# Three gate units of each layer moved from the search stage into the stage of the key scores

## What is computed

```python
h = x @ w_in                                   # (1024, 1024) @ (1024, IN_WIDTH), split in 14 parts
sc = einsum('bqhd,bsd->bqhs', qi, ki)          # key search: 8 index heads of width 64, 1024 keys
idx_score = einsum('bqhs,bqh->bqs', relu(sc), wi)
_, idx = lax.top_k(where(causal, idx_score, -inf), 256)
...                                            # attention over the 256 keys found, two further attentions
mixed = concatenate([a, bo, co]) * silu(gate)  # gate: 1024 columns of h
out = mixed @ w_out;  x = layer_norm(ALPHA * x + out)
```

## Time and profile before

| | us |
|---|---|
| median of 3 runs (lowest, highest) | 3095.87 (3090.37, 3101.58) |
| the profiled execution, its span | 3091.31, 3089.6 |
| PE busy (share of the span) | 2838.9 (92%) |
| DVE busy | 1642.1 (53%) |
| ACT busy | 984.2 (32%) |
| POOL busy | 792.1 (26%) |
| score stage, layer 1 and 2 (1475.3 to 1541.8, 2344.8 to 2411.3) | 66.5, 66.5 |
| search stage, layer 1, from its first product to its last | 261.3 |

### The profile page before, as it was taken

One profiled execution on the slowest core, in us unless ns is written; L12 is line 12 of the kernel. 1 busy time (PEld: TensorE's weight loads), 2 busy tenths in 40 slices (PEclk: granted clock), 3 DMA queues, 4 the chain that ended last, 5 costly groups with the idle time before them and its releaser, 6 DMA issues. The chain is left out here.

```text
span 3089.6 us, 39183 instructions
## 1 busy us (share of the span) xinstructions
PE 2838.9 (92%) x14936; PEld 2312.0 (75%) x14936; DVE 1642.1 (53%) x2808; ACT 984.2 (32%) x1911; POOL 792.1 (26%) x510
## 2 busy tenths in 40 slices
PE   5999888989999999989699989988898899999988
PEld 4777687778888888868378878776685688778767
DVE  4270476533224224233799536676435996265866
ACT  3150454121001001110574034564104660244741
POOL 2233103213333333423033351002131233340021
PEclk9999898999999999999999999999899999999999
DMA  3101002111121121132032520005320224300042
GB/s 111 38 31 51 2 1 87 61 36 44 38 69 38 39 68 48 41 134 55 9 113 92 139 101 1 1 1 174 127 64 11 96 96 123 136 1 1 1 137 96
DMA packets 83146, 194.07 MB, mean 63 GB/s; under 512 B 15488, under 2 KB 34448, under 8 KB 81936
## 3 DMA queue, kind: packets, MB, share of 16 engines
q1 hardware_dynamic: 71056, 153.78, 14.9%
q10 hardware_dynamic: 11904, 37.76, 4.0%
HBM read 141.18 MB, written 33.55 MB: 57 GB/s over the span
## 5 line engine op out<-in xcount | busy, mean ns | idle before, releaser
L344 PE MATMUL psum<-H,ffn_W 128*128 128x512 f32 x672 | 262.9, 391 | 4.8 <-DVEq L1716 3.1
L345 PE MATMUL psum<-H,ffn_W 128*128 128x512 f32 x672 | 262.4, 390 | 0.0
L346 PE MATMUL psum<-H,ffn_W 128*128 128x512 f32 x672 | 262.4, 390 | 0.0
L344 PE MATMUL psum<-H,tk_W 128*128 128x512 f32 x640 | 249.2, 389 | 0.4 <-POOL tk_W L2045 0.4
L346 PE MATMUL psum<-H,tk_W 128*128 128x512 f32 x640 | 249.0, 389 | 0.0
L345 PE MATMUL psum<-H,tk_W 128*128 128x512 f32 x640 | 249.0, 389 | 0.0
L1483 POOL CAST ffn_W<-ffn_W 128x1024 fp32r<-128x1024 f32 (+1 forms) x77 | 65.1, 846 | 471.3 <-PE psum L346 469.1
L1963 DVE TENSOR_SCALAR_CACHE_REDUCE MB<-OM,tk_mid 128x512 bf16<-128x512 f32 (+2 forms) x192 | 184.3, 1010 | 2.3
L1931 ACT ACTIVATE MB<-OM,tk_mid 128x384 bf16<-128x384 f32 (+2 forms) x192 | 157.2, 820 | 74.0 <-DVE tk_mid L1960 73.2
L2043 POOL CAST tk_W<-tk_W 128x1024 fp32r<-128x1024 f32 (+1 forms) x56 | 54.3, 970 | 482.7 <-PE psum L346 331.4
L1697 DVE TENSOR_SCALAR ffn_Y<-ffn_G,ffn_par 128x1024 f32<-128x1024 f32 x21 | 21.1, 1004 | 288.6 <-ACT ffn_G L1670 288.6
(11 more groups left out here) (443 smaller groups left out, 7193.7 us busy)
## 6 DMA issues: line engine op xcount, KB each, us to landing
tk_W<-in_w_feat SPq DMA_DIRECT2D x40, 512.0 KB, 3.6
ffn_W<-in_ffn_w_gate SPq DMA_DIRECT2D x21, 512.0 KB, 3.6
ffn_W<-in_ffn_w_val SPq DMA_DIRECT2D x21, 512.0 KB, 3.5
ffn_W<-in_ffn_w_down SPq DMA_DIRECT2D x42, 256.0 KB, 2.6
OM<-in_w_feat SPq DMA_DIRECT2D x16, 512.0 KB, 7.3
OM<-MB ACTq DMA_DIRECT2D x64, 128.0 KB, 2.4
GATE<-OM ACTq DMA_DIRECT2D x16, 512.0 KB, 3.3
OM<-OM ACTq DMA_DIRECT2D x64, 128.0 KB, 3.3
```

The costliest lines, as they stand in the source:

```text
L344: pe.matmul(out, a1, b1, start=start, stop=False)
L345: pe.matmul(out, a1, b2, start=False, stop=False)
L346: return pe.matmul(out, a2, b1, start=False, stop=stop)
```

## The change

Three of the eight gate units are no longer made in the search stage. The score stage gets them: SP loads their three weight tiles ahead of the small parameters, POOL splits them, and PE does a unit's 48 matmuls in 16 chunks of three, put behind score steps of at most 512 keys (two heads each). The scores use six single banks (three steps in flight in place of two pairs of heads), the unit the fourth pair. ACT bends each step by itself, and after the step behind a unit's last chunk it takes the unit's Silu and sends it to DRAM; PE's next unit waits for that Silu. In the search stage DVE puts the selection of one query tile behind each of the first six rotary units; the swap of halves has one buffer pair instead of two.

```diff
+GATES_BESIDE = 3

-def index_stage(kit, IQ, VS, IS, AM, causal, prepare):
+def index_stage(kit, IQ, VS, IS, AM, causal, prepare, XT, rest, items, staged, GATE, first):
-    SLOTS = 4
+    H, SLOTS, PAIRS, PARTS, UNIT_PAIR, CHUNKS = 8, 4, 3, 2, 3, 2 * KT
+    U = len(items)
...
+    steps = [(t, h, c) for t in range(NT) for h in range(0, H, 2) for c in range(0, P * (t + 1), HALF)]
+    bent_by = [2 * max(s for s, (tt, hh, _) in enumerate(steps) if (tt, hh) == (t, h - h % 2)) + h % 2 + 1
+               for t, h in heads]
+    share = [end_of(t, c) - c for t, h, c in steps[:-4]]
+    upto, last_step, n = [], [], 0
+    for s in range(len(steps)):
+        while n < min(CHUNKS * U, CHUNKS * U * sum(share[:s + 1]) // sum(share)):
+            if n and n % CHUNKS == 0 and s < last_step[-1] + 2:
+                break
+            n += 1
+            if n % CHUNKS == 0:
+                last_step.append(s)
+        upto.append(n)
...
             def _(sp):
+                for i, src in enumerate(items):
+                    if i >= PARTS:
+                        sp.wait_ge(split, i - PARTS + 1)
+                    sp.dma_start(W[:, i % PARTS, :], src).then_inc(w_in[i % PARTS], 16)
                 prepare.load(sp)
+            @block.gpsimd
+            def _(pool):
+                for i in range(U):
...
+                    pool.tensor_copy(w1, w).then_inc(rounded, 1)
+                    pool.wait_ge(rounded, i + 1)
+                    pool.tensor_tensor(w2, w, w1.bitcast(FP32), ALU.subtract).then_inc(split, 1)
...
+                def chunk(n):
+                    u, c, k = n // CHUNKS, n % CHUNKS // KT, n % KT
+                    if n % CHUNKS == 0:
+                        pe.wait_ge(split, u + 1)
+                        if u:
+                            pe.wait_ge(copied, u)
...
+                    last = three_products(pe, kit.pair(UNIT_PAIR)[:, at], w1, w2, XT[:, k, at], rest[:, k, at],
+                                          k == 0, k == KT - 1)
...
+                for s, (t, h, c) in enumerate(steps):
+                    e = end_of(t, c)
+                    if s >= PAIRS:
+                        pe.wait_ge(bent, 2 * (s - PAIRS) + 2)
+                    for m in range(2):
+                        rows = slice(64 * m, 64 * m + 64)
+                        pe.matmul(kit.psum[:, 2 * (s % PAIRS) + m, 0:e - c], IQ[rows, h // 2, t * P:(t + 1) * P],
+                                  IQ[rows, 4, c:e], start=True, stop=True).then_inc(scored, 1)
+                    for n in range(upto[s - 1] if s else 0, upto[s]):
+                        chunk(n)
...
+                        act.activation(R[:, j % SLOTS, c:e], kit.psum[:, 2 * (s % PAIRS) + m, 0:e - c], ACT.Relu
+                                       ).then_inc(bent, 1)
+                    for u in range(U):
+                        if s == last_step[u] + 1:
+                            act.wait_ge(products, u + 1)
+                            if u >= 2:
+                                act.wait_ge(kept[u % 2], 16 * (u // 2))
+                            act.activation(staged[u % 2], kit.pair(UNIT_PAIR), ACT.Silu).then_inc(copied, 1)
+                            act.wait_ge(copied, u + 1)
+                            act.dma_start(GATE[:, first + u, :], staged[u % 2]).then_inc(kept[u % 2], 16)
...
-                        dve.wait_ge(bent, j + 1)
+                        dve.wait_ge(bent, bent_by[j])
...
-def search_stage(kit, XT, rest, items, topk, staged, partner, rot, fox, GATE, FQD, rope, DQD, DV):
+def search_stage(kit, XT, rest, items, topk, staged, fox, GATE, FQD, rope, DQD, DV):
-    n_pairs, SLOTS, PARTS, RING, TURNS = 3, 2, 2, len(staged), 2
+    n_pairs, SLOTS, PARTS, RING, TURNS = 3, 2, 2, 3, 1
-    FOX, GATES, ROPES = len(fox), KT, 8
+    FOX, GATES, ROPES = len(fox), KT - GATES_BESIDE, 8
...
+        partner, rot, third = (sbuf(nc, mem, f"tk_{n}", [P, 1, S]) for n in ("partner", "rot", "third"))
+        turned = staged[0:2] + [third[:, 0, :]]
...
                 topk.search(dve)
-                topk.select(dve)
...
                     if n:
                         add_partner(n - 1)
+                    if n < NT - TOPK // P:
+                        topk.select(dve, TOPK // P + n)
                 add_partner(ROPES - 1)
```

More of the change, by code:

```diff
@@ L1854, in _ @@
             @block.tensor
             def _(pe):
[L1856 to L1869, removed]
+                def chunk(n):
[4 more added lines that the diff above has]
+                            pe.wait_ge(copied, u)
+                    w1, w2 = (a[:, u % PARTS, k * P:(k + 1) * P] for a in (W1, W2))
+                    at = slice(c * HALF, (c + 1) * HALF)
+                    last = three_products(pe, kit.pair(UNIT_PAIR)[:, at], w1, w2, XT[:, k, at], rest[:, k, at],
+                                          k == 0, k == KT - 1)
+                    if n % CHUNKS == CHUNKS - 1:
+                        last.then_inc(products, 1)
@@ L1871, in _ @@
             @block.scalar
             def _(act):
[L1873 to L1878, removed]
+                for s, (t, h, c) in enumerate(steps):
+                    e = end_of(t, c)
+                    for m in range(2):
+                        j = t * H + h + m
+                        act.wait_ge(scored, 2 * s + m + 1)
+                        if j >= SLOTS:
+                            act.wait_ge(added, j - SLOTS + 1)
+                        act.activation(R[:, j % SLOTS, c:e], kit.psum[:, 2 * (s % PAIRS) + m, 0:e - c], ACT.Relu
[8 more added lines that the diff above has]
+                            act.dma_start(GATE[:, first + u, :], staged[u % 2]).then_inc(kept[u % 2], 16)
@@ L1880, in _ @@
+                for n, sem in enumerate(kept):
+                    act.wait_ge(sem, 16 * len(range(n, U, 2)))
             @block.vector
@@ L1974, in search, with select @@
         own.then(dve.tensor_tensor(hi, hi, mid, ALU.max))
-        self.own, self.T0 = own, T0
-    def select(self, dve):
-        MB, IS, own, T0, N = self.MB, self.IS, self.own, self.T0, 3
+        self.own = own
+    def select(self, dve, t):
+        MB, IS, own, N = self.MB, self.IS, self.own, 3
         lo, hi = self.lo, self.hi
@@ L1982, in select @@
         B, R, last, left = self.B, self.R, self.last, self.left
[L1983 to L1999, removed]
@@ L2002, in search_stage @@
-def search_stage(kit, XT, rest, items, topk, staged, partner, rot, fox, GATE, FQD, rope, DQD, DV):
+        n = P * (t + 1)
+        on_act = t in self.ON_ACT
+        m = (self.ON_ACT if on_act else self.ON_DVE).index(t)
+        low, high = (a[:, N * on_act:N * on_act + N] for a in (lo, hi))
+        s = IS[:, self.keys(t)]
+        own(dve.tensor_scalar(A[:, 0:n], s, high[:, m:m + 1], 0.0, ALU.is_gt if on_act else ALU.is_ge, ALU.add,
+                              accum_out=last[:, m:m + 1]))
@@ new lines, in select @@
+        own.wait()
+        own(dve.tensor_scalar(left[:, m:m + 1], last[:, m:m + 1], -1.0, float(TOPK), ALU.mult, ALU.add))
+        own.then(dve.scalar_tensor_tensor(B[:, 0:n], s, low[:, m:m + 1], A[:, 0:n], ALU.is_ge, ALU.subtract))
+        own.then(dve.tensor_tensor_scan(R[:, 0:n], self.one.to_broadcast([P, n]), B[:, 0:n], 0.0,
+                                        ALU.mult, ALU.add))
+        own.then(dve.scalar_tensor_tensor(B[:, 0:n], R[:, 0:n], left[:, m:m + 1], B[:, 0:n],
+                                          ALU.is_le, ALU.mult))
@@ L2007, in search_stage @@
+        own.then(dve.tensor_tensor(A[:, 0:n], A[:, 0:n], B[:, 0:n], ALU.add))
+        own.then(dve.tensor_scalar(MB[:, self.keys(t)], A[:, 0:n], 1.0, -NEG, ALU.subtract, ALU.mult))
+def search_stage(kit, XT, rest, items, topk, staged, fox, GATE, FQD, rope, DQD, DV):
     nc = kit.nc
-    n_pairs, SLOTS, PARTS, RING, TURNS = 3, 2, 2, len(staged), 2
+    n_pairs, SLOTS, PARTS, RING, TURNS = 3, 2, 2, 3, 1
     WIDE_ORDER = (4, 5, 6, 7, 0, 1, 2, 3)
-    FOX, GATES, ROPES = len(fox), KT, 8
+    FOX, GATES, ROPES = len(fox), KT - GATES_BESIDE, 8
@@ L2097, in _ @@
                         act.wait_ge(added, n)
-                        act.dma_start(DQD[:, n - 1, :], staged[(n - 1) % RING]).then_inc(put[(n - 1) % RING], 16)
+                        act.dma_start(DQD[:, n - 1, :], turned[(n - 1) % RING]).then_inc(put[(n - 1) % RING], 16)
                 for n, t in enumerate(WIDE_ORDER):
@@ L2124, in _ @@
                         dve.wait_ge(put[n % RING], 16 * (n // RING))
-                    own(dve.scalar_tensor_tensor(staged[n % RING], out, scale, cos, ALU.mult, ALU.mult))
+                    own(dve.scalar_tensor_tensor(turned[n % RING], out, scale, cos, ALU.mult, ALU.mult))
                     if n >= TURNS:
@@ L2888, in layer @@
     IS = flat[:, 0:KEYS]
-    index_stage(kit, IQ, VS, IS, AM, causal, prepare)
+    room = flat[:, KEYS:]
+    staged = [room[:, n * S:(n + 1) * S] for n in range(2)]
```

(2 more changed lines are left out.)

26 lines of the change are left out of this document (18 added, 8 removed).

## The result

| | us |
|---|---|
| changed, median of 16 runs (lowest, highest) | 3100.99 (3093.58, 3106.43) |
| before, median of 16 runs beside them | 3092.73 (3088.96, 3102.08) |
| ratio | 1.0021, 95% interval 1.0011 to 1.0031 |
| changed, span of the profiled execution | 3098.7 (before 3089.6) |
| PE busy, changed | 2861.5 (92%) |

The change costs 0.2%. That is within the 0.3% I had called no change, but on the other side of the 12 us of gain that I forecast; it lies at the very end of the stated range (3060 to 3101), which reaches that far only by the 8 us for scatter added to rival B's 3093. Again the windows by stage say where it is. First the changed kernel's, of layer 1: score stage, products of the search stage, then three pieces of the score stage.

What follows compares the result with a forecast made beforehand. Score stage taken as DVE-bound, search stage as PE-bound. The score stage grows 26.5 us, the search stage gives back 32.7: 6.2 less per layer, 12 for two, from 3094.8 to 3083 us; range 3060 to 3101.

Steps and rivals of the forecast that it cites:

- rival B: Chance 0.20: gain lost to waits at the search stage's wide product or a lower PE clock at score start; 3093.
- DVE's timetable: Search stage: DVE frees the banks in time, so PE's wait was put at 0, bounds 0 to 5 us per layer.
- The wait at the start: Score stage: the first chunk waits for SP's tile and POOL's split, 7.3 us, with three score steps inside.
- the sum: PE's path through the changed score stage, from its first score to DVE's end: 91.4 us, against 64.9 before.
- The tail: Score stage: DVE's work behind PE's last score, between 5.3 and 10.2 us, taken as 7.5.
- item 3: Score stage: PE changing between 64 and 128 rows, 0.28 us per group of chunks, 9.5 us for 34 groups.
- item 4: Score stage: second and third unit wait for ACT's Silu, 2.8 us the first time, 1.5 the second, 4.3 together.
- Rival C: Chance 0.13: weight loads can't run ahead at a change of rows, 0.66 us per group; 14 us slower, 3109.
- A: Chance 0.17: changes of rows in the score stage are hidden under other work; 31 us gained, 3064.
- C's break-even: Score stage: the cost per group of chunks from which the change would be slower, 0.46 us.

Runs made afterwards that it cites:

- the run with 3064: Changed kernel with the first gate tile loaded and split in the stage ahead, and chunks behind every fourth score step only (11 groups): 3064.01 us, ratio 0.9880.
- with four: Four gate units moved instead of three, first gate tile loaded and split in the stage ahead, chunks behind every fourth score step: 3088.6 us, ratio 0.9951.
- the early tile: Changed kernel with the first gate tile loaded and split at the end of the stage ahead: 3084.08 us, ratio 0.9959.
- the first experiment: Changed kernel with chunks behind every third score step only, 15 groups in place of 34, as many products: 3084.0 us, ratio 0.9965.
- the second comparison: The changed kernel measured once more, unaltered, against the kernel before: 3104.56 us, ratio 1.0010 (0.9996 to 1.0024).

## Why the prediction was wrong

**Right.** The search stage: 1,008 products without a gap, 228.4 us, and DVE's timetable held (with three units, and 1.1 us to spare at the last banks in the run with 3064; with four DVE was late). The wait at the start: first product 7.1 us behind the first score, 7.3 in the sum. ACT's Silu starts 0.01 us behind the end of the table load, so the 1.3 us of the row held. The Trainium skill (ScalarE: Activation LUTs, What ACT_TABLE_LOAD costs) gives 1.38 us more for draining; this trace doesn't show them either. The tail: 7.5 forecast; PE's last score ends at 1565.8, DVE at 1573.4.

**Wrong: item 3, the change of rows.** "0.09 + 0.10 + 0.09 = 0.28 us for one group" lacked a fourth part of 0.11, and each of the three was 0.10: 0.41. Over 34 groups this is 13.9 us in place of 9.5, 4.4 us per layer. The count of groups was right, and it makes this the largest loss in the stage: it was in the sum as something given, where it is the one number that the author of the order is free to choose.

**Wrong: the weight given to rival B.** The clock did fall in the 7 us wait, and stayed at half until 1488.2: 2.4 us in layer 1, and 3.2 in layer 2 with the second stretch there. I had left it at nothing in the forecast and priced it at up to 6.8 in the rival. The forecast argued from DVE's pace that PE would catch up; but the stage was about to become PE's, and nothing lost by the bound is caught up.

**Too high: item 4, Silu.** The starts around the two waits lie 2.69 and 1.70 us apart where 0.53 is usual behind such a pass, so they cost 2.2 and 1.2 us, 3.4 where the sum had 4.3. This error went the other way and hid a part of the first two.

With these three the sum reads 7.1 + 30.1 + 32.7 + 13.9 + 3.4 + 7.5 + 2.4 = 97.1 us, and 97.7 lie between PE's first score and DVE's end (1475.66 to 1573.37); 0.6 us stay unplaced. The first two corrections have their own experiments (15 groups, 11 roughly; the early tile).

**Rival C** was wrong in its price: a group costs 0.41 us, not 0.66. Its mechanism isn't refuted. In steady work the load for the next product starts 0.23 us ahead of it; at the change the trace has it start with its product, and the load for the second product 0.11 later:

```profile
1532.89 0.19 PEld L347 LDWEIGHTS psum<-H,ix_W 128*128 128x128 f32 x1 [0.76 <-issue]
1533.00 0.19 PEld L348 LDWEIGHTS psum<-H,ix_W 128*128 128x128 f32 x1
```

No run parts the drain from the loads, so what makes up the 0.41 stays open; that it is paid per group is shown. C's break-even, 0.46 us per group, was the right way to look at it: 0.41 for the groups and 2.4/34 = 0.07 for the clock make 0.48, beyond that point, and the change is slower. **A** is refuted by the first experiment.

**What stays open.** The stages account for +2.1 us. The timed difference is 8.3 us (ratio 1.0011 to 1.0031, 3.4 to 9.6 us) in the first comparison, 3.0 in the second, whose interval reaches from -1.2 to 7.4. In the first traces the parts behind the products differ by +7.7 us. But the same parts took 945.6 and 955.7 us in two traces of the kernel before, and between 945.6 and 963.9 over all traces, with between 72 us (in the shortest) and 106 us of that time at half clock. Over the 13 traces the two rise together, the length by about 0.4 us for each microsecond at half clock, and the first pair differs by 20 us at half clock (72 and 92); so the +7.7 goes with the clock, which fell for longer still (99 us) in the second trace of the kernel before. The +2.1 agrees with the second comparison and with the second pair of traces (3099.6 and 3100.7); whether some microseconds beyond it belong to the change I can't tell.

## What to carry to other kernels

Before work is interleaved, count how many times the two kinds change, not only how much is moved: here 34 groups of a sound idea cost 13.9 us per layer, 11 groups of the same products 4.5 by the same price, and that with the first weight tile fetched in the stage before turned 0.2% slower into 1.2% faster. Idle time of an engine in a stage bound by another can be filled only up to the point where it becomes the bound; from there each microsecond moved in is paid in full, and every small loss with it, so find that point unit by unit (one unit cost 5 us and saved 11; in the best version a third cost 9 and saved 14 to 15, 11 by its products and the rest by the order of the banks, and a fourth cost 9 and saved at most 1.5). And a resource that is freed in one place (PE in the search stage) has its next limit close by: look for it before moving the unit that reaches it.

## What the runs showed of the hardware

- One turn from 128 rows to 64 and back costs PE 0.41 us at full clock, in four parts: 0.10 in the first pass of scores, 0.10 at the step from scores to products, 0.11 at the second product, 0.10 at the return to scores. The Trainium skill (TensorEngine Tiling (Array Packing), Key Properties) says that a change of tiling drains TensorE; the parts at the changes agree with it but don't prove it. The late second instruction stands behind plain stops as well (0.53 us between score passes at 1526.56, 0.34 between products at 1549.22, in the kernel before), so it isn't a matter of the rows alone.
- PE's granted clock was 0.50 from 1478.0 to 1488.2, over most of a stop of 6.2 us and the 5.4 us of work behind it, and 1.00 throughout the same place when the stop was gone. The stop and the clock together cost 8.7 us, 1.4 times the stop. The waits of 2.1 us for a first Silu were followed by half clock in some layers (1504.7 to 1508.0 with the early tile, at a price of 1.5 us) and not in others.
- The kernel before, traced twice, differed by 10 us in span while its score stages and its products agreed to 0.1 us. Differences below that are read from the stages, not from two spans.
